# Gates and projections of a first block with tokens on partitions and 512 moving columns, the merged tile turned back by transposes

## The reference

```python
for l in range(DEPTH):
    h = rmsnorm(x, pre_norm_g[l])
    (u, v, z_a, c_q, c_kv, k_rope, z_b, x_c, z_c, g_a, g_b, g_c) = jnp.split(h @ w_in[l], cuts, axis=-1)
    y_a = gmlp_spatial(u, v, ...) * silu(z_a)          # 256 x 1024
    y_b = mla_attention(c_q, c_kv, k_rope, ...) * silu(z_b)   # 256 x 1024
    y_c = rg_lru(x_c, ...) * silu(z_c)                 # 256 x 1280
    merged = (sigmoid(g_a) * (y_a @ w_proj_a[l])
              + sigmoid(g_b) * (y_b @ w_proj_b[l])
              + sigmoid(g_c) * (y_c @ w_proj_c[l]))
    x = x + rmsnorm(merged @ w_out[l], post_norm_g[l])
```

## Time and profile before

| | us |
|---|---|
| runs | 1603.38, 1600.79, 1595.78 |
| median of the three | 1600.79 |
| the profiled execution's own time | 1603.51 |
| its span | 1601.7 |
| PE busy | 1500.8 (94%) |
| DVE busy | 1053.1 (66%) |
| ACT busy | 874.3 (55%) |
| mean granted clock | 0.972 |

### The profile page before, as it was taken

How to read it: one execution, slowest core, us unless ns; L and a number is a source line. 1 busy time by engine, 2 the same in 40 slices (tenths; PEclk the granted TensorE clock), 3 DMA queues, 4 the chain that set the end, 5 groups by cost and what they waited for, 6 DMA issues and landing times.

```text
span 1601.7 us, 25719 instructions
## 1 busy us (share of the span) xinstructions
PE 1500.8 (94%) x10589; PEld 1410.6 (88%) x10589; DVE 1053.1 (66%) x1626; ACT 874.3 (55%) x1541; POOL 88.7 (6%) x141
## 2 busy tenths in 40 slices
PE   6998999999989989999999899999999888899997
PEld 6998889999989888899999799987998777899876
DVE  5645559886766366698868678855566434688744
ACT  6465557564554646564645666644566333566544
POOL 9100000006000000000000100000000000000000
PEclk9999999999999999999999999999899798999998
DMA  7524366566646143665666455565343011565561
GB/s 220 160 73 138 106 197 183 163 185 171 216 134 171 46 137 109 207 185 168 184 195 210 141 183 184 171 190 165 106 124 118 14 40 54 171 184 184 172 197 66
DMA packets 214692, 241.14 MB, mean 151 GB/s; under 512 B 19240, under 2 KB 185282, under 8 KB 214576
## 3 DMA queue, kind: packets, MB, share of 16 engines
q1 hardware_dynamic: 208672, 228.66, 47.8%
q0 software_dynamic: 5904, 10.85, 2.5%
HBM read 238.42 MB, written 1.05 MB: 150 GB/s over the span
## 4 chain that ended last, share of the span: by engine, by line
PE 79%; DVE 9%; ACT 6%; DMA 3%; issue 2%; POOL 0%; DVEq 0%; POOLq 0%
PE bank L589 23%; PE bank L593 22%; PE bank L592 22%; DVE w_lo L1642 2%; PE bank L688 2%; PE bank L760 2%; ACT w_hi L1160 2%; PE bank L1062 1%; DMA raw<-in_ffn_up 1%; ACT S L1328 1%; DMA raw<-in_w_in 1%; PE bank L1048 1%; PE bank L964 1%; DMA raw<-in_mla_w_ukv 1%; PE bank L788 1%
## 5 line engine op out<-in xcount | busy, mean ns | idle before, releaser
L1642 DVE TENSOR_TENSOR w_lo<-raw,w_hi 128x1024 fp32r<-128x1024 f32 (+2 forms) x460 | 523.8, 1154 | 296.2 <-ACT w_hi L1160 293.9
L589 PE MATMUL bank<-h_hi,w_hi 128*128 128x256 f32 (+1 forms) x2024 | 577.7, 285 | 21.1 <-DVE w_lo L1642 5.9
L1160 ACT CAST w_hi<-raw 128x1024 fp32r<-128x1024 f32 (+2 forms) x460 | 453.5, 991 | 244.7 <-DMA raw<-in_w_in 89.8
L592 PE MATMUL bank<-h_lo,w_hi 128*128 128x256 f32 (+1 forms) x2024 | 575.4, 284 | 0.0
L593 PE MATMUL bank<-h_hi,w_lo 128*128 128x256 f32 (+1 forms) x2024 | 575.3, 284 | 0.0
L589 PEld LDWEIGHTS bank<-h_hi,w_hi 128*128 128x128 f32 (+1 forms) x2024 | 390.1, 193 | 23.2 <-issue 17.9
L593 PEld LDWEIGHTS bank<-h_hi,w_lo 128*128 128x128 f32 (+1 forms) x2024 | 390.0, 193 | 0.0
L592 PEld LDWEIGHTS bank<-h_lo,w_hi 128*128 128x128 f32 (+1 forms) x2024 | 389.9, 193 | 0.1
L589 PE MATMUL bank<-w_hi,h_hi 128*128 128x512 f32 (+1 forms) x272 | 104.6, 384 | 12.9 <-DVEq L2386 10.2
L592 PE MATMUL bank<-w_lo,h_hi 128*128 128x512 f32 (+1 forms) x272 | 102.9, 378 | 0.0
L593 PE MATMUL bank<-w_hi,h_lo 128*128 128x512 f32 (+1 forms) x272 | 102.7, 378 | 0.0
(11 more groups left out here) (353 smaller groups left out, 2396.5 us busy)
## 6 DMA issues: line engine op xcount, KB each, us to landing
raw<-in_w_in SPq DMA_DIRECT2D x160, 512.0 KB, 3.8
raw<-in_ffn_up SPq DMA_DIRECT2D x88, 512.0 KB, 3.6
raw<-in_ffn_down SPq DMA_DIRECT2D x40, 512.0 KB, 4.4
raw<-in_w_proj_a SPq DMA_DIRECT2D x16, 512.0 KB, 3.4
raw<-in_w_proj_b SPq DMA_DIRECT2D x16, 512.0 KB, 3.4
raw<-in_w_out SPq DMA_DIRECT2D x16, 512.0 KB, 4.6
raw<-in_ple_gate SPq DMA_DIRECT2D x16, 512.0 KB, 3.8
raw<-in_w_proj_c SPq DMA_DIRECT2D x16, 384.0 KB, 3.3
```

The costliest lines, as they stand in the source:

```text
L589: first = pe.matmul(out_, lh, rh, start=start, stop=False)
L592: pe.matmul(out_, lh, rl, start=False, stop=False)
L1160: act.copy(w_hi[b][:, 0:size], raw[b][:, 0:size]).then_inc(sems["hi_done"], 1)
L1642: dve.tensor_tensor(w_lo[b][:, 0:size], raw[b][:, 0:size], w_hi[b][:, 0:size].bitcast(F32), ALU.subtract).then_inc(sems["w_split"], 1)
```

## The change

ga, a, gb, b, gc and c are computed in the second way, with tokens on partitions. PE uses `wide_square` (and `half_wide` around the spatial matmuls); the slots become 4 k-tiles x 512 columns, and c's slots are 2, 4 and 4 k-tiles for each half of the columns (`PROJ_C`). SP loads them in the same order. ACT's gate does both slots' four casts of a half first and then two sigmoids of 512 columns into `G_t`; DVE merges 512 columns at a time in `m_t`. Because out needs merged with features on partitions, `turn_merged` on PE transposes it back, eight 128 x 128 blocks into two K banks for each half, ACT copies the high part from PSUM (`high_merged`) and DVE subtracts for the low part (`low_merged`). The first half is turned inside c's second half, ahead of its last slot. The second half is turned inside out, behind the first half of its first slot (two k-tiles). The transposes of `p_in` stand behind that turn.

```diff
-        out += [(8, 256)] * 4 + [(4, 512)] * 4 + [(8, 256)] * 28 + [(5, 256)] * 8 + [(4, 512)] * 4
+        out += [(8, 256)] * 4 + [(4, 512)] * 4 + [(8, 256)] * 8 + [(4, 512)] * 20
+        out += ([(2, 512)] + [(4, 512)] * 2) * 2 + [(4, 512)] * 4
...
+PROJ_C = [(0, 2), (2, 4), (6, 4)]
...
@@ sync @@
-                square("ga", w_in, COL_GA)
...
+                wide_square("ga", w_in, COL_GA)
+                wide_square("a", ins["w_proj_a"], 0)
+                wide_square("gb", w_in, COL_GB)
+                wide_square("b", ins["w_proj_b"], 0)
+                wide_square("gc", w_in, COL_GC)
+                for n in range(2):
+                    for j, (k, tiles) in enumerate(PROJ_C):
+                        load(j, rows_of(ins["w_proj_c"], l, k * P, tiles, n * 512, 512))
+                    w.go("S", 3)
...
@@ tensor @@
-                half_square(0, h)
+                def half_wide(act):
+
+                    for k in range(2):
+                        tokens(k, 0, act, k0=4 * k, start=k == 0, stop=k == 1)
+                    w.go("S", 2), w.go("J", 2)
+                half_wide(h)
...
-                half_square(1, h)
+                half_wide(h)
                 w.go("y_ready", 2 * KT)
...
+                def turn_merged(n):
+
+                    pe.wait_ge(sems["m_f"], w.taken("m_f", 2))
+                    for u in range(2):
+                        transposes([m_t[:, t, (4 * n + 2 * u + f) * P:(4 * n + 2 * u + f + 1) * P]
+                                    for f in range(2) for t in range(TT)])
+                for n in range(2):
+                    for j, (k, tiles) in enumerate(PROJ_C):
+                        if n == 1 and j == 2:
+                            turn_merged(0)
+                        tokens(j, 2 * n, (yc_hi, yc_lo), k0=k, start=j == 0, stop=j == 2,
+                               ready=None if n else "yc_ready", tiles=LT)
+                    w.go("S", 3)
+                w.go("J", 4)
                 w.go("m_ready", KT)
+                tokens(0, 0, h, stop=False, ready="m_ready", only=(0,))
+                turn_merged(1)
                 if l == L - 1:
                     pe.wait_ge(sems["p_in_done"], 16)
                     for n in range(L):
                         transposes([p_in[:, n, t, f * P:(f + 1) * P] for f in range(2) for t in range(TT)])
-                wide_square("out", h, "m_ready")
+                tokens(0, 0, h, stop=False, ready="m_ready", only=(1,))
+                tokens(1, 0, h, k0=4, start=False, ready="m_ready")
+                w.go("S", 2), w.go("J", 2)
+                half_wide(h)
...
@@ scalar @@
                 def gate(label, tile0):
-                    for i in range(2):
...
+                    for n in range(2):
+                        if label == "ga" and n == 1:
                             high_ya()
...
+                        for k in range(2):
+                            hi(k, 0), hi(k, 1)
+                            if k == 0 and tile0 is not None:
+                                root_yc(n, tile0)
+                        for t in range(TT):
+                            evac("J", t, G_t[:, t, n * 512:(n + 1) * 512], ACT.Sigmoid, width=512)
                         if tile0 is not None:
-                            high_yc(i, tile0)
-                        w.go("S", 2), w.go("J", 4)
+                            high_yc(n, tile0)
+                        w.go("S", 2), w.go("J", 2)
...
+                def high_merged(n):
+
+                    for u in range(2):
+                        b = w.bank("K", u)
+                        act.wait_ge(full[b], w.turn("K", u))
+                        k = 4 * n + 2 * u
+                        act.copy(h_hi[:, k:k + 2, :].rearrange("p a n -> p (a n)"), ps[b][:, :])\
+                            .then_inc(sems["m_hi_done"], w.given("m_hi_done"))
+                    w.go("K", 2)
...
+                for n in range(2):
+                    for j in range(3):
+                        if n == 1 and j == 2:
+                            high_merged(0)
+                        hi(j, 0), hi(j, 1)
+                    w.go("S", 3)
+                w.go("J", 4)
                 evacuated_all()
...
                 for n in range(2):
+                    if n == 0:
+                        high_merged(1)
...
                     hi(0, 0), hi(0, 1), hi(1, 0), hi(1, 1)
...
@@ vector @@
+                def set_merged(n, t):
+                    b = w.bank("J", t)
+                    cols = slice(n * 512, (n + 1) * 512)
+                    dve.wait_ge(full[b], w.turn("J", t))
+                    dve.tensor_tensor(m_t[:, t, cols], G_t[:, t, cols], ps[b][:, :], ALU.mult).then_inc(free[b], 1)
...
+                    dve.tensor_tensor(both, G_t[:, t, cols], ps[b][:, :], ALU.mult).then_inc(free[b], 1)
+                    dve.wait_ge(free[b], w.turn("J", j) + 1)
+                    return dve.tensor_tensor(m_t[:, t, cols], m_t[:, t, cols], both, ALU.add)
...
+                def add_last(n):
+
+                    for t in range(TT):
+                        add_merged(n, t, 2 * n + t).then_inc(sems["m_f"], w.given("m_f"))
+                        dve.wait_ge(sems["m_f"], w.value("m_f"))
+                for j in range(3):
+                    lo(j, 0), lo(j, 1)
+                add_last(0)
+                w.go("S", 3)
+                lo(0, 0), lo(0, 1), lo(1, 0), lo(1, 1)
+                low_merged(0)
+                lo(2, 0), lo(2, 1)
+                add_last(1)
+                w.go("S", 3), w.go("J", 4)
+                low_merged(1)
```

More of the change, by code:

```diff
@@ L638, in queries, with tokens @@
                                 mm.then_inc(sems[f"full{bank}"], 1)
-            def tokens(j, job, act, k0=0, start=True, stop=True, ready=None, tiles=KT):
+            def tokens(j, job, act, k0=0, start=True, stop=True, ready=None, tiles=KT, only=(0, 1)):
                 slot = w.n["S"] + j
@@ L644, in tokens @@
                 banks = [w.bank("J", job + t) for t in range(TT)]
-                if start:
+                if start and 0 in only:
                     for t, bank in enumerate(banks):
                         pe.wait_ge(free[bank], w.turn("J", job + t))
-                for half, (ka, kb) in enumerate(halves(k_tiles)):
+                for half in only:
+                    ka, kb = halves(k_tiles)[half]
                     b = half_ready(slot, half)
@@ L2015, in three_d @@
-                def three_d(b):
-                    return acc(b).rearrange("p (a n) -> p a n", a=1)
-                def set_merged(i, k):
-                    b = w.bank("J", k)
-                    dve.wait_ge(full[b], w.turn("J", k))
-                    t = dyn(i, 4, k)
-                    dve.tensor_tensor(m[:, t, :], G[:, t, :], three_d(b), ALU.mult).then_inc(free[w.bank("J", k)], 1)
-                def add_merged(i, k, j=None):
-                    j = k if j is None else j
+                            begin(dyn(n, 1, tile0))
@@ new lines, in with_recurrence @@
+                        for k in range(2):
+                            lo(k, 0), lo(k, 1)
+                            if k == 0 and tile0 is not None:
+                                finish(dyn(n, 1, tile0))
+                        for t in range(TT):
+                            evacuate(n, t)
+                        if tile0 is not None:
+                            last(dyn(n, 1, tile0))
+                        w.go("S", 2), w.go("J", 2)
+                def set_merged(n, t):
[3 more added lines that the diff above has]
+                    dve.tensor_tensor(m_t[:, t, cols], G_t[:, t, cols], ps[b][:, :], ALU.mult).then_inc(free[b], 1)
@@ L2026, in add_merged @@
+                def add_merged(n, t, j=None):
+                    j = t if j is None else j
                     b = w.bank("J", j)
+                    cols = slice(n * 512, (n + 1) * 512)
+                    both = hf[:, :, :].rearrange("p a n -> p (a n)")
                     dve.wait_ge(full[b], w.turn("J", j))
-                    t = dyn(i, 4, k)
-                    dve.tensor_tensor(hf[:, k % 2:k % 2 + 1, :], G[:, t, :], three_d(b), ALU.mult)\
-                        .then_inc(free[w.bank("J", j)], 1)
@@ L2031, in add_merged, with low_merged @@
-                    dve.wait_ge(free[w.bank("J", j)], w.turn("J", j) + 1)
-                    return dve.tensor_tensor(m[:, t, :], m[:, t, :], hf[:, k % 2:k % 2 + 1, :], ALU.add)
-                none = lambda i, k: None
+                    dve.tensor_tensor(both, G_t[:, t, cols], ps[b][:, :], ALU.mult).then_inc(free[b], 1)
+                    dve.wait_ge(free[b], w.turn("J", j) + 1)
+                    return dve.tensor_tensor(m_t[:, t, cols], m_t[:, t, cols], both, ALU.add)
+                def low_merged(n):
+                    for u in range(2):
+                        b = w.bank("K", u)
+                        k = 4 * n + 2 * u
+                        dve.wait_ge(sems["m_hi_done"], w.taken("m_hi_done"))
```

(7 more changed lines are left out.)

102 lines of the change are left out of this document (21 added, 81 removed).

## The result

| | before | changed |
|---|---|---|
| median, first comparison (6 and 6 runs) | 1600.67 | **1589.30** (1585.91 to 1592.07) |
| ratio, 95% interval | | 0.9931 [0.9912, 0.9951] |
| the profiled execution's time and span | 1603.51, 1601.7 | 1585.91, 1584.1 |
| mean granted clock | 0.972 | 0.978 |
| DMA packets | 214692 | 188954 |

The kernel is 11.4 us faster, and 1591.0 was forecast. Two later comparisons of the same pair gave 5.6 and 7.6 us. The stages that the change touches account for 7.5 us, and this figure came back in all three traces of the changed kernel; the rest is scatter, and most of it goes with the granted clock, as is shown further down.

A forecast was written before the change was run, and what follows sets the result against it. PE, busy 94% of the span, bounds the kernel, and only each matmul's fixed 11 to 20 ns can be saved. The terms sum to 4.9 us a layer, 9.8 for two: 1591.0 against the median 1600.8; range 1583.5 to 1600.5.

The forecast's parts named there:

- products with h: Gates ga, gb, gc: 576 matmuls at 0.1203 us become 288 at 0.2271, saving 3.9 us a layer.
- products with y: Products a, b, c: 312 wide matmuls at an assumed 0.230 us save 1.7 us a layer, ends 2.6 and 0.7.
- ya starts earlier: At the spatial products: casts ahead of sigmoids move ya tiles 1.4 us earlier, saving 0.75 us beyond the steps.
- wait at gc: At gc's start: PE's 1.4 us wait for a bank goes, banks being freed a half earlier; other end 0.
- transposes: 16 added of 128 x 128 a layer, all on PE's path, cost 1.75 us; bounds 1.6 and 5.6.
- stand before the second turn, start to start: In out: PE waits 1.1 us for the merge, queued behind a w_out split on VectorE; ends 0 and 3 us.
- The Trainium skill's rule: For 600 pairs of narrow matmuls made wide: 1.6 us a layer saved instead of 5.6, landing between rivals B and C.
- rival B: Products with y save 0.7 us, PE stands 3 us before the second turn: 2.0 us a layer, 1596.8 us; 18%.
- rival D: Tail: a late split of w_out's second slot lets PE cool down, 3.4 us a layer slower, 1607.6 us; 6%.
- Rival C: Fixed part belongs to stationary loads or reads, so wide matmuls save nothing: -0.7 us a layer, 1602.2 us; 6%.
- rival A: Products with y save 2.6 us and the tail costs nothing: 7.1 us a layer, 1586.6 us; 18%.

The follow-up runs named there:

- same_row: Changed kernel with 192 bytes of unused space per partition ahead of the overlay tiles, moving ya, yb, yc and y2; 1583.31 us, ratio 0.9912 to the kernel before.
- cast_first: Kernel before the change, with both weight slots' casts ahead of a gate's four 256-column sigmoids on ScalarE; one run, 1610.78 us against 1604.69.
- merge_first: Changed kernel with VectorE's last merge ahead of the split of the second piece of w_out's second slot; 1586.87 us, ratio 0.9935 to the kernel before.
- merge_256: Changed kernel with each of DVE's gate multiplications and additions cut into two pieces of 256 columns; one run, 1590.15 us.
- after_third: Changed kernel timed again without any edit; 1590.04 us, ratio 0.9949 to the kernel before.

## Why the prediction was right

The mechanism came as forecast. By its own sum for a layer, in us:

| term | forecast | measured |
|---|---|---|
| products with h | 3.9 | 3.8 |
| products with y | 1.7 | 0.6 |
| ya starts earlier | 0.75 | 0.9 |
| wait at gc | 1.4 | 1.1 |
| transposes | -1.75 | -1.8 |
| stand before the second turn, start to start | -1.1 | -0.9 |
| sum | 4.9 | 3.7 |

The measured terms add up to what the layer shows by its own ends, 172.8 - 169.1 = 3.7.

**Products with h.** 21.89 + 21.79 + 21.84 us for ga, gb and gc, against 69.3. The step was known from the output product and held.

**Products with y.** This is the term that was mis-sized. The prediction took 0.230 between 0.2271 and 0.2333, since nothing said which row the three resemble. It was 0.2333, that of y2. There was a sign, unread: y and h already differed in the narrow form, 0.1178 against 0.1203, so the tile's name mattered and y2 was the relative of ya, yb and yc. `same_row` shows that the place in SBUF is the reason.

**The Trainium skill's rule** ("TensorE: Matmul & The Clock Gate", section Back-to-back issue gap), N/2.4 + 2.5 ns, would have given an estimated 1.6 us for the 600 pairs. The traces disagree with it: they gave 3.8 + 0.6. For the products with y alone the saving is near the rule's 2.6 ns a pair (2 x 0.1178 - 0.2333 = 0.0023 us), though both steps lie above the rule's. The same section's sustained figure of about 131 ns at 512 columns is not reached by any product here; the lowest was 226.7 ns.

**ya and its casts.** 6.56 us from the first spatial matmul to ga's second half became 5.69. `cast_first` shows the order as the cause. What the prediction didn't see is that in the narrow kernel this order costs more than it gives: the first layer of the one run is 2.3 us longer by it.

**The wait at gc.** Gone but for 0.3 us of issue time, for the reason given (banks by half). DVE's merges were to become 0.6 us shorter a half. By start times four merges of 256 columns took 3.64 us (two of them from 363.18 to 365.00), two of 512 take 2.88 (357.74 to 360.62): 0.8 less, so this remark held.

**Transposes and tail.** The turns cost 0.79 and 0.85 and the longer step behind each. The merge ended 18.5 us into c's second half (404.41 to 422.9), and 18.4 was forecast; PE's own work before the turn reached 17.6 instead of 17.3 (60 steps of y are 0.2 us longer), and so the stand was 0.9 instead of 1.1. Its cause, the split of the last piece of w_out's second slot queued ahead of the merge, is shown by `merge_first`. w_out's pieces landed in a median of 3.7 us, not 4.6, so rival B's transfers and rival D's late piece didn't come; the clock behind the turn stayed at 1.00. Rival C is excluded by the steps, rival A by the y step and the stand. Rival B was half right: its y step is the one that came, and only its 3 us of stand did not. Rival A's total has a slip: its terms add up to 6.9 us a layer, not 7.1, and its time to 1587.0, not 1586.6; the range hardly moves by it.

**The total.** The layers' 3.7 + 3.75 = 7.5 us would be 1593.2, and 1589.3 came. The 1.7 us between forecast and result is no proof of the sum: a sum 1.2 us a layer too high, 1.1 of it in the products with y, was offset by a comparison with 3.9 us of luck. Over three comparisons the gain was 11.4, 5.6 and 7.6, on average 8.2.

## What to carry to other kernels

Wider moving columns saved the fixed part of each matmul here and nothing more: count instructions, and take both steps from the same kernel's rows. When an operand changes from moving to stationary, look at where its tile lies relative to the weights in a line of 256 bytes; 192 bytes of padding brought as much here as the whole rewrite, though 3.4 of its 7.4 us came in stages that the rewrite doesn't touch. It wasn't tried on the kernel before, whose narrow y products lie at their cheap place already. A reordering on one engine can gain in one kernel and lose in another that has no bank to spare: test it apart from the edit that it came with. And when two kernels differ by a few microseconds, read the stages and the granted clock of each run beside the times.

## What the runs showed of the hardware

- A fp32r matmul of 512 columns takes 0.2267 us from start to start with stationary and moving tile at the same place modulo 256 bytes, 0.2333 with the stationary one 64 bytes above, 0.2289 with it 64 below. With 256 columns and the activation moving, 64 above is the better (0.1178 against 0.1203).
- Eight transposes of 128 x 128 in float32 take 0.79 us from their first start to the next matmul's in a stream (the first turn; p_in), 0.85 behind a stand of 0.74 us.
- Two DVE operations of 256 columns in a row cost only 0.06 us more than one of 512 (0.74 to 0.76 against 0.68 to 0.69, `merge_256`). In the merges of the kernel before, where one multiplication and one addition of 256 columns take turns, each costs 0.45 us from start to start.
- The granted clock fell behind the same 2.3 us wait in one execution (`after_third`) and not in another (`same_row`). Between the layers three further spells make 264.3 us on average, one 261.6, none 259.7.
- Over the runs of these kernels 0.01 of mean granted clock goes with 11.7 us of 1590.
